# Decode states in a hybrid GLA/HGRN2 decoder step: value rows spread from four row strips of TensorE, answers with the state as moving side in four column strips, norms on rows

## The reference, cut to what matters

```python
def _gated_linear_recurrence(q, k, v, log_a, s0):
    '''Per-token causal recurrence S_t = diag(a_t) S_{t-1} + k_t^T v_t, o_t = q_t S_t, in chunkwise form.'''
...
oa = _rmsnorm(oa, gla_norm_w) * jax.nn.silu(ga.reshape(B, L, GLA_HEADS, GLA_DV).astype(f32))
...
ob = _rmsnorm(ob, hgrn_norm_w) * jax.nn.sigmoid(gb.reshape(B, L, HGRN_HEADS, HGRN_DV).astype(f32))
ya = jnp.einsum('ble,ed->bld', oa.reshape(B, L, GLA_V).astype(h.dtype), w_proj_a)
yb = jnp.einsum('ble,ed->bld', ob.reshape(B, L, HGRN_V).astype(h.dtype), w_proj_b)
merged = jax.nn.sigmoid(ua) * ya + jax.nn.sigmoid(ub) * yb
```

## Time and profile before

| | |
|---|---|
| median of 3 runs | 2134.78 us (2134.27 to 2140.59) |
| span of the profiled execution, first to last instruction; it has no other time | 2141.0 us |
| busy: PE, DVE, ACT, POOL | 2037.1, 698.1, 446.6, 415.6 us |
| P0 to S (729.60 to 873.92 us) | 144.32 us, PE busy 144.30, mean granted clock 0.72 |

### The profile page before, as it was taken

How to read it: one execution, slowest core, us unless ns; L and a number is a source line. 1 busy time by engine, 2 the same in 40 slices (tenths; PEclk the granted TensorE clock), 3 DMA queues, 4 the chain that set the end, 5 groups by cost and what they waited for, 6 DMA issues and landing times.

```text
span 2141.0 us, 24545 instructions
## 1 busy us (share of the span) xinstructions
PE 2037.1 (95%) x7690; PEld 1275.7 (60%) x7690; DVE 698.1 (33%) x1481; ACT 446.6 (21%) x940; POOL 415.6 (19%) x657
## 2 busy tenths in 40 slices
PE   6999999989999999999997989999999999999994
PEld 1754558577767677888876644444444444444443
DVE  0113970697169722100126621111111111111114
ACT  1203431443134322000001111111111111111111
POOL 0001430253024200000000332222222222222220
PEclk9999999999999877899997899999999999999997
DMA  8112341211210351232011569999999999999962
GB/s 376 39 44 114 126 160 40 79 43 42 79 40 3 150 187 59 80 118 79 9 40 38 197 265 362 365 377 365 364 373 367 364 366 371 364 369 371 366 198 90
DMA packets 56942, 419.51 MB, mean 196 GB/s; under 512 B 6289, under 2 KB 10001, under 8 KB 31145
## 3 DMA queue, kind: packets, MB, share of 16 engines
q1 hardware_dynamic: 33689, 339.44, 39.7%
q0 software_dynamic: 21456, 78.10, 14.0%
q10 hardware_dynamic: 1728, 1.05, 0.2%
HBM read 362.96 MB, written 55.61 MB: 195 GB/s over the span
## 4 chain that ended last, share of the span: by engine, by line
PE 81%; DVE 8%; DMA 3%; ACT 3%; issue 3%; POOL 1%; POOLq 0%; SPq 0%; DVEq 0%; ACTq 0%
PE ps L1006 22%; PE ps L870 12%; PE ps L1028 11%; PE ps L836 8%; PE ps L821 6%; PE ps L997 3%; PE ps L900 3%; PE ps L767 2%; DVE work L1391 2%; PE ps L457 2%; PE ps L855 2%; PE ps L848 1%; DVE Xb L1398 1%; PE ps L793 1%; PE ps L967 1%
## 5 line engine op out<-in xcount | busy, mean ns | idle before, releaser
L1006 PE MATMUL ps<-W,work 128*128 128x512 f32 x1168 | 514.9, 594 | 1.6 <-ACT work L1185 1.2
L1006 PEld LDWEIGHTS ps<-W,work 128*128 128x128 f32 x1168 | 216.8, 191 | 247.2 <-issue 247.2
L1028 PE MATMUL ps<-work 128*128 128x512 f32 x576 | 259.1, 592 | 0.0
L1717 DVE SCALAR_TENSOR_TENSOR work<-ps,work 128x256 f32<-128x256 f32 x73 | 35.3, 484 | 513.2 <-ACT work L1191 513.2
L836 PE MATMUL ps<-Hb,W 128*128 128x260 f32 x768 | 173.5, 390 | 0.0
L1028 PEld LDWEIGHTS ps<-work 128*128 128x128 f32 x576 | 103.8, 190 | 103.3 <-issue 103.3
L836 PEld LDWEIGHTS ps<-Hb,W 128*128 128x128 f32 x768 | 148.8, 194 | 24.2 <-ACT work L1090 0.7
L1727 DVE COPY work<-ps 128x512 f32<-128x512 f32 x144 | 99.6, 692 | 182.7 <-PE ps L1028 93.6
L1220 POOL TENSOR_TENSOR work<-work 128x128 f32<-128x128 f32 x168 | 83.0, 526 | 388.7 <-ACT work L563 388.7
L1283 POOL DMA_INDIRECT ffrows<-work x72 | 115.7, 1607 | 188.4 <-DVE work L1727 159.1
L821 PE MATMUL ps<-W,Hb 128*128 128x512 f32 (+1 forms) x320 | 138.4, 593 | 0.0
(11 more groups left out here) (253 smaller groups left out, 2270.4 us busy)
## 6 DMA issues: line engine op xcount, KB each, us to landing
W<-wexp SPq DMA_DIRECT2D x74, 2048.0 KB, 8.8
work<-wexp SPq DMA_DIRECT2D x73, 1024.0 KB, 8.2
W<-wq SPq DMA_DIRECT2D x36, 2048.0 KB, 8.1
work<-st_in SPq DMA_DIRECT2D x8, 1024.0 KB, 7.9
st_out<-work SPq DMA_DIRECT2D x8, 1024.0 KB, 6.2
Xb<-xT SPq DMA_DIRECT2D x2, 2080.0 KB, 17.4
h2rows<-work SPq DMA_DIRECT2D x5, 512.0 KB, 2.8
yT<-Xb SPq DMA_DIRECT2D x2, 1040.0 KB, 5.4
```

What stands on the lines that cost most here:

```text
L1006: mm = pe.matmul(ps[:, k % 2, :], xe[:, k % 2, c, :], GU[:, k % 4, c, :], start=(c == 0), stop=(c == KC - 1))
L1028: mm = pe.matmul(ps[:, 4 + hf, :], aT[:, k % 2, f, :], WD[:, k, f, hf * 512:(hf + 1) * 512], start=(f == 0), stop=(f == 1))
```

## The change

Four edits go together. The value rows of the decode tokens, four quarters of 512, no longer lie side by side on partitions 0 to 7 but on partitions 0, 32, 64 and 96 on (`v_rows`), so each of a spread's four matmuls reads another strip of 32 rows of TensorE. The answers change sides: the new state is now the moving operand, and the weights are 32 columns of queries (`qrows`) that hold sequence b's query in column b and zeros elsewhere; head h goes to column strip h % 4, into a third of PSUM bank 4 by h // 4, and the eight sequences add up there, since sequence b fills row 32 g + b only. The norm then works on rows: ScalarE squares and sums each part along its columns, GpSimd makes the inverse root by a power, ScalarE copies with that scale, and S becomes four transposes back to columns, behind which VectorE applies the gates. GpSimd zeroes `qrows` and VectorE places the queries in it before the stage.

```diff
-        Vs = Xb[0:DEC, 0:2048]
-        sq_, sk_, sa_ = (view(Xb, 2048 + 96 * k, 96, "p (h b) -> p h b", b=DEC) for k in range(3))
+        Vs = view(Xb, 0, 512)
+        sq_, sk_, sa_ = (view(Xb, 512 + 96 * k, 96, "p (h b) -> p h b", b=DEC) for k in range(3))
+        qrows = view(Xb, 1088, 12 * DEC * 32, "p (h n) -> p h n", h=12)
...
-        oS = view(work, 12288, 128, "p (j b) -> p j b", b=DEC)
-        oS2 = view(work, 12416, 128, "p (j b) -> p j b", b=DEC)
-        oms = view(work, 12544, 128, "p (j b) -> p j b", b=DEC)
+        oS = view(work, 12288, 512)
+        osum, orms = view(work, 15920, 4), view(work, 15924, 4)
+        osq = view(work, 15936, 256)
+        PARTS = [(0, 256), (256, 128), (384, 128)]
...
+        def v_rows(gi, a, b):
+
+            lo = 0 if b < 4 else 32 * (a if gi == 0 else 1 + gi)
+            return slice(lo, lo + min(P, NT - b * P))
...
-            sp.wait_ge(s_sn2, 6)
+            sp.wait_ge(s_sn2, 2)
...
+                    lo = v_rows(gi, a, b).start
                     for c in range(KC):
-                        mm = pe.matmul(ps[0:rows, bank, :], H[:, c, b * P:b * P + rows], ring[:, q % 4, :, c, :],
+                        mm = pe.matmul(ps[lo:lo + rows, bank, :], H[:, c, b * P:b * P + rows], ring[:, q % 4, :, c, :],
...
                 pe.wait_ge(s_sn, 12 * (b + 1))
-                for j in range(16):
-                    h = j // 2 if j < 8 else j - 4
-                    mm = pe.matmul(ps[:, 4, DEC * j + b:DEC * j + b + 1], snew[:, b % 2, j * P:(j + 1) * P],
-                                   sq_[:, h, b:b + 1], start=True, stop=True)
+                if b == 0:
+                    pe.wait_ge(s_qrow, 2)
+                for h in range(12):
+                    g = h % 4
+                    lo, hi = (h * GV, (h + 1) * GV) if h < GH else (1024 + (h - 4) * HV, 1024 + (h - 3) * HV)
+                    at = PARTS[h // 4][0]
+                    mm = pe.matmul(ps[32 * g:32 * g + 32, 4, at:at + hi - lo], qrows[:, h, 32 * b:32 * b + 32], snew[:, b % 2, lo:hi],
+                                   start=(b == 0 and h < GH), stop=(b == DEC - 1 and h >= 8))
                 mm.then_inc(s_sop, 1)
 
             def spread(b):
                 for j in range(4):
                     since(pe, s_sn, 12 * (b - 1) + (2, 4, 8, 12)[j])
-                    pe.matmul(ps[:, j, :], ident[0:DEC, b:b + 1].broadcast_to([DEC, P]), Vs[:, j * 512:(j + 1) * 512],
+                    lo = 32 * j
+                    pe.matmul(ps[:, j, :], ident[lo:lo + DEC, lo + b:lo + b + 1].broadcast_to([DEC, P]), Vs[lo:lo + DEC, :],
                               start=True, stop=True).then_inc(s_vb, 1)
...
                 elif what == "S":
-                    pe.wait_ge(s_sn2, 2)
-                    pe.matmul(ps[:, 4, 128:256], ones, oS2.rearrange("p j b -> p (j b)"), start=True, stop=True).then_inc(s_sop, 1)
+                    pe.wait_ge(s_dsc, 3)
+                    for c in range(4):
+                        mm = pe.transpose(ps[:, 0, c * P:(c + 1) * P], oS[:, c * P:(c + 1) * P], ident)
+                    mm.then_inc(s_dtr, 1)
...
-                elif what == "N2":
-                    act.wait_ge(s_sn2, 4)
-                    act.activation(oms.rearrange("p j b -> p (j b)"), oms.rearrange("p j b -> p (j b)"), ACT.Sqrt).then_inc(s_lng, 1)
+                elif what == "N1":
+                    act.wait_ge(s_sop, DEC)
+                    for k, (at, w) in enumerate(PARTS):
+                        since(act, s_dsq, k)
+                        act.activation(osq[:, 0:w], ps[:, 4, at:at + w], ACT.Square, accum_out=osum[:, k:k + 1]).then_inc(s_dsq, 1)
+                    act.wait_ge(s_drt, 3)
+                    for k, (at, w) in enumerate(PARTS):
+                        act.activation(oS[:, at:at + w], ps[:, 4, at:at + w], ACT.Copy, scale=orms[:, k:k + 1]).then_inc(s_dsc, 1)
...
+            pool.wait_ge(s_rec, 3)
+            pool.memset(view(Xb, 1088, 12 * DEC * 32), 0.0).then_inc(s_qrow, 1)
+            pool.wait_ge(s_dsq, 3)
+            for k, (lo, hi, v) in enumerate(((0, 1, GV), (1, 3, HV))):
+                pool.tensor_scalar(osum[:, lo:hi], osum[:, lo:hi], 1.0 / v, EPS, ALU.mult, ALU.add).then_inc(s_drt, 1)
+            pool.wait_ge(s_drt, 2)
+            pool.tensor_tensor(orms[:, 0:3], osum[:, 0:3], C("mhalf").broadcast_to([P, 3]), ALU.pow).then_inc(s_drt, 1)
...
+            dve.wait_ge(s_qrow, 1)
+            dve.tensor_copy(qrows[:, :, 0:DEC * 33 - 32:33], sq_).then_inc(s_qrow, 1)
...
-            def norm_first():
-                dve.wait_ge(s_sop, 8)
-                dve.tensor_copy(oS.rearrange("p j b -> p (j b)"), ps[:, 4, 0:128]).then_inc(s_sn2, 1)
-                dve.wait_ge(s_sn2, 1)
-                dve.tensor_tensor(oS2, oS, oS, ALU.mult).then_inc(s_sn2, 1)
-
             def norm_rest():
-                dve.wait_ge(s_sop, 9)
-                sums = ps[:, 4, 128:256].rearrange("p (j b) -> p j b", b=DEC)
-                dve.tensor_copy(oms, sums).then_inc(s_sn2, 1)
-                dve.wait_ge(s_sn2, 3)
-                pair = oms[:, 0:8, :].rearrange("p (h k) b -> p h k b", k=2)
-                both = oS2[:, 0:8, :].rearrange("p (h k) b -> p h k b", k=2)
-                for k in range(2):
-                    ins = dve.tensor_tensor(both[:, :, k, :], pair[:, :, 0, :], pair[:, :, 1, :], ALU.add)
-                ins.then_inc(s_mod, 1)
-                dve.wait_ge(s_mod, 1)
-                dve.tensor_scalar(oms[:, 0:8, :], oS2[:, 0:8, :], 1.0 / GV, EPS, ALU.mult, ALU.add).then_inc(s_mod, 1)
-                dve.tensor_scalar(oms[:, 8:16, :], oms[:, 8:16, :], 1.0 / HV, EPS, ALU.mult, ALU.add).then_inc(s_sn2, 1)
-                dve.wait_ge(s_mod, 2)
-                dve.wait_ge(s_lng, 1)
-                dve.reciprocal(oms, oms).then_inc(s_mod, 1)
-                dve.wait_ge(s_mod, 3)
-                dve.tensor_tensor(oS, oS, oms, ALU.mult).then_inc(s_mod, 1)
-                dve.wait_ge(s_mod, 4)
+                dve.wait_ge(s_dtr, 1)
                 dve.wait_ge(s_hw, 5)
-                dve.tensor_tensor(oa[:, :, SEQ:NT], oS[:, 0:8, :], gdec[:, 0:8, :], ALU.mult).then_inc(s_sn2, 1)
-                dve.tensor_tensor(ob[:, :, SEQ:NT], oS[:, 8:16, :], gdec[:, 8:16, :], ALU.mult).then_inc(s_sn2, 1)
-                dve.wait_ge(s_sn2, 6)
+                turned = ps[:, 0, :].rearrange("p (k g r) -> p k g r", k=4, g=4)[:, :, :, 0:DEC]
+                dve.tensor_tensor(oa[:, :, SEQ:NT].rearrange("p (g k) b -> p k g b", k=2), turned[:, 0:2],
+                                  gdec[:, 0:8, :].rearrange("p (g k) b -> p k g b", k=2), ALU.mult).then_inc(s_sn2, 1)
+                dve.tensor_tensor(ob[:, :, SEQ:NT].rearrange("p (k g) b -> p k g b", k=2), turned[:, 2:4],
+                                  gdec[:, 8:16, :].rearrange("p (k g) b -> p k g b", k=2), ALU.mult).then_inc(s_sn2, 1)
+                dve.wait_ge(s_sn2, 2)
```

More of the change, by code:

```diff
@@ L222, in decoder_step @@
         s_vb, s_sa, s_sn, s_sop = sem("v_bcast"), sem("s_scaled"), sem("s_new"), sem("s_o")
-        s_sn2 = sem("sample_norm")
+        s_sn2 = sem("sample_gated")
+        s_qrow = sem("q_rows")
+        s_dsq, s_drt, s_dsc, s_dtr = sem("sample_squares"), sem("sample_root"), sem("sample_scaled"), sem("sample_turned")
         s_g1, s_g2, s_g3, s_g5 = sem("gate_proj"), sem("gate_tanh"), sem("gate_value"), sem("gate_applied")
@@ L638, in layer_norm_dve @@
             for hf, (lo, hi) in enumerate(halves):
-                dve.wait_ge(s_lng, 2 + 2 * which + hf)
+                dve.wait_ge(s_lng, 1 + 2 * which + hf)
                 dve.reciprocal(lnr[:, NT + lo:NT + hi], lnr[:, lo:hi]).then_inc(s_ln, 1)
@@ L864, in product @@
                 if hf:
-                    pe.wait_ge(s_sn2, 6)
+                    pe.wait_ge(s_sn2, 2)
                 if k >= 3:
@@ L1082, in _ @@
                 if what == "v":
[L1083 to L1086, removed]
+                    rows = v_rows(gi, a, b)
+                    dst = V[:, b, a * 512:(a + 1) * 512] if b < 4 else Vs[rows, :]
+                    act.activation(dst, ps[rows, bank, :], ACT.Copy).then_inc(s_zev, 1)
                 elif what == "gl":
@@ L1528, in _ @@
                     merged(k)
-                elif what == "N1":
-                    norm_first()
                 elif what == "N2":
```

## The result

The changed kernel takes 2074.24 us (median, 2070.47 to 2077.70), the kernel before 2135.78 in the same set: ratio 0.9726, 95% interval 0.9704 to 0.9747.

A forecast was written before the change was run, and what follows sets the result against it. TensorE was taken to bound the stage from P0 to S, partly at a low clock. Terms 7.7 + 2.5 + 11.8 + 0.7 + 30.6 - 0.9 = 52.4 us gave 2083 us, own range 2075 to 2092, wide range 2064 to 2126.

The forecast's parts named there:

- signs of being wrong: Trace signs: a spread of 3.6 us or 1.1, products still taking 6 us, TensorE waiting for VectorE's state passes.
- What bounds the stage: From P0 to S, TensorE is busy for 144.30 of 144.32 us, so its time is the kernel's, one for one.
- The spread: Decode spreads B2 to B7: four matmuls in 5 slots, 2.14 us in place of 3.42, saving 7.7 us.
- all four strips side by side: Rival: records of different strips overlap however queued, spreads and answers 0.86 us each, so 2065 us; chance 0.13.
- The answers: Decode answers A0 to A7: 2.3 us each in place of 3.78, saving 11.8 us, plus 0.7 for shared edges.
- B0 and B1: First two spreads, the second waiting for VectorE's state 0: P1 can start 2.5 us earlier but stays slow.
- The clock: TensorE's granted clock from A0 to P12: new answers keep it up, 30.6 of 33.6 us regained, 3 still lost.
- The norm: S waits behind P12 for the chain on ScalarE and GpSimd: a loss of 0.9 us, at most 1.4.
- At nothing: Costs put at nothing: zeroing padded queries, moved value-projection rows, and heavier state traffic and VectorE load, both staying hidden.
- no overlap: Rival: strips don't overlap, spreads keep their cost, answers take 3.93 us; only 12 us gained, 2123 us; chance 0.22.
- slow clock: Rival: the clock stays at 1.2 GHz from A0 on, 17 us more, 2152 us; chance 0.04.
- Clock falls at nearly every item: Rival: strips overlap but the clock falls as before; 2096 us with half of 33.6 lost, 2113 with all; chance 0.15.

The follow-up runs named there:

- B1 behind P1: The changed kernel with ORDER's two-item slots moved so that the second spread runs after product P1 instead of before it: 2073.94 us, ratio 0.9730.
- one strip for all spreads: The changed kernel with the four matmuls of each spread all reading the rows of strip 0: 2094.93 us, ratio 0.9835.
- the second trace: The changed kernel run again, unchanged, in one set with the two orders of weight loads: 2071.05 us, ratio 0.9720.

## Why the prediction came out as it did

The time lies in the range, but the range was wide (2064 to 2126), and the forecast of 2083 was missed by 9 us. Two errors of opposite sign met in it: the strips overlap more than forecast, which is worth some 15 us, and a wait that no step has costs about 8 with the low clock behind it. Without the wait the time would have been near 2066, at the edge of the range; that the forecast came as near as it did is luck. Two of its own signs of being wrong were seen, a spread of 1.1 us and a wait for VectorE's state passes in B3.

- **What bounds the stage** held: TensorE is busy for 79.08 of 81.98 us, and what the stage lost the kernel lost.
- **The spread** was mis-sized. The step that failed is "a matmul's second record needs its own strip's first to be through, and the next strip's first record can only start beside that second one". The first half is so. The second is not: neighbouring strips' first records start before any second one. A spread streams 0.86 us, not 2.14, and the term 7.7 was 6 x 2.56 = 15.4. This is the rival *all four strips side by side*, to which 0.13 was given; its 2065 and 8 us for the wait make 2073. The Trainium skill, "TensorE: Matmul & The Clock Gate", Part 3, has 3.07 times for four row strips; here a spread with its edges went from 3.63 to 1.07 us, 3.4 times. The same part says that matmuls start strictly in program order. For float32 matmuls in different strips the records here start out of it (a strip's first record ahead of another's second, and in the strip-major answers a strip's first matmul ahead of another's third), and the measurement decides.
- **The answers** likewise: 1.01 us an item and 0.3 more for the edge of the product ahead, in place of 3.78, is 8 x 2.46 = 19.7 us where 11.8 and 0.7 stood. The 0.3 is counted from P9's 3.39, which ends at the first weight load of A5, taken ahead; in the stretch behind the stage 16 records take 3.5 us (171.02 us for 783), so that the edge itself is nearer 0.2.
- **B0 and B1**: 2.2 us, 2.5 forecast. P1 stayed slow, as forecast, and B1 behind P1 showed why.
- **The clock** held in mechanism: 32.0 us came back in the stage, and from A0 to P12, where 30.6 of 33.6 were forecast, 30.2. That the sizes agree so closely is in part luck: the 3 us still lost were to be lost at the short spreads, and lie in P4 behind the wait (3.0) instead. Its reasons held: new answers do not take the clock down (one strip for all spreads), few-row spreads of 3.6 us do (six of six there, but not B6 before), full-row ones don't, and the short ones of 1.07 us don't where the answers are the new ones.
- **The norm** cost 0.45 us, 0.9 forecast.
- **At nothing** failed in one clause: "State traffic rises from 0.38 of the DMA engines' time to 0.6 in a stretch of 92 us [...]; both stay hidden". A mean share says nothing of one transfer's place in its queue. The write-out of state 0 stands behind 4 MB of weights, and the stage now reaches the passes that need it before it lands: 4.8 us in B3 and 3.0 in P4, about 8 us, 6 in the second trace.

With both sizes right and the wait counted the sum would have been 15.4 + 2.5 + 19.7 + 30.6 - 0.5 - 4.8 = 63, close to the 62.3 measured in the stage (the 3.0 in P4 are part of the 3 that the clock term leaves out).

The rivals *no overlap* and *slow clock* fell outright. *Clock falls at nearly every item* fell as well: from A0 on only P4 did, behind the wait.

## What to carry to other kernels

Small matmuls in different strips of the array run side by side, float32 with its two records too, if the strips alternate in the program: the same twelve matmuls took 1.0 us strip by strip in turn and 2.4 us strip-major. When a stage on one engine is to become much shorter, go through every transfer whose end that stage waits for and ask what stands ahead of it in its queue; a mean busy share hides it. And work on few rows of the matrix engine can be paid for twice, in itself and in the clock of the full product behind it, as with spreads of 3.6 us over 8 rows here, while as many columns over 128 rows left the clock alone. So it is worth measuring both, the item and the product behind it, before and after.

## What was not expected of the hardware

- Matmul records of different strips start ahead of earlier ones in the program, but only of near ones: three records were overtaken in the strip-major answers.
- Behind a spread of 3.62 us over 8 rows the product had a granted clock of 0.68, so part of it ran at 1.2 GHz; behind one of 3.43 us over 128 rows, with as many columns, it had 1.00, 2.4 GHz throughout. The first was seen behind B2 to B7 with one strip for all, but not behind B6 of the kernel before; the second behind all spreads over all rows.
